# Expert outputs scattered without accumulation and summed at the end, and the first block's down projection moved one expert later

## What is computed

```
scores = sigmoid(xf @ w_router)
_, idx = top_k(masked(scores + router_bias), TOP_K)         # 8 of 64 experts per token
wts = sel / sum(sel) * ROUTED_SCALE
def body(acc, blk):                                         # tok, w: the slots of one expert; e: the expert
    xb = x_pad[tok]
    yb = ((silu(xb @ w_gate[e]) * (xb @ w_up[e])) @ w_down[e]) * w[:, None]
    return acc.at[tok].add(yb), None
h = h + routed + shared                                     # h: the residual stream
h = h + (p_i @ w_ple_proj) * sigmoid(rmsnorm(h) @ w_ple_gate)
y = rmsnorm(h)
```

## Time and profile before

| | us |
|---|---|
| median of three runs (lowest, highest) | 1949.45 (1948.63, 1951.06) |
| the profiled execution | 1950.84 |
| its span, first to last instruction | 1949.0 |
| PE busy in the span | 1740.4 |
| DVE, ACT, POOL busy | 885.6, 785.5, 572.5 |
| mean granted TensorE clock, as a share of full speed | 0.951 |

### The profile page before, as it was taken

One profiled execution on the slowest core, in us unless ns is written; L12 is line 12 of the kernel. 1 busy time (PEld: TensorE's weight loads), 2 busy tenths in 40 slices (PEclk: granted clock), 3 DMA queues, 4 the chain that ended last, 5 costly groups with the idle time before them and its releaser, 6 DMA issues. The chain is left out here.

```text
span 1949.0 us, 24720 instructions
## 1 busy us (share of the span) xinstructions
PE 1740.4 (89%) x7154; PEld 1086.3 (56%) x7155; DVE 885.6 (45%) x1566; ACT 785.5 (40%) x1453; POOL 572.5 (29%) x668
## 2 busy tenths in 40 slices
PE   6999999978883989898999998999998989786998
PEld 4666666536772556465555655655555556452443
DVE  3333334316994543554444445444455443552333
ACT  2222222213330554564554555545555454551221
POOL 0011000002554332443333334334334242441010
PEclk9999999978996999999999998999999999897999
DMA  9200000022114889999999899999899898984001
GB/s 357 92 0 0 0 0 0 27 81 110 65 65 145 255 277 270 298 296 297 271 272 293 256 278 324 275 264 297 254 312 305 250 285 253 302 264 137 33 22 38
DMA packets 122124, 371.34 MB, mean 191 GB/s; under 512 B 18674, under 2 KB 33970, under 8 KB 121677
## 3 DMA queue, kind: packets, MB, share of 16 engines
q1 hardware_dynamic: 86021, 257.30, 36.2%
q0 software_dynamic: 35760, 113.69, 24.9%
q10 hardware_dynamic: 320, 0.07, 0.0%
HBM read 298.86 MB, written 74.01 MB: 191 GB/s over the span
## 5 line engine op out<-in xcount | busy, mean ns | idle before, releaser
L1406 PE MATMUL Y<-raw_d,hT 128*128 128x512 f32 (+1 forms) x768 | 367.1, 624 | 20.6 <-ACT hT L1466 19.5
L191 DVE TENSOR_TENSOR lo_gu<-raw_g,hi_gu 128x1024 fp32r<-128x1024 f32 x130 | 154.6, 1223 | 399.5 <-ACT hi_gu L184 399.3
L1322 POOL DMA_INDIRECT acc_dram<-y,to_row x128 | 215.2, 1681 | 402.9 <-ACT y L1474 315.0
L1364 PE MATMUL GU<-hi_gu,x_hi 128*128 128x512 f32 (+1 forms) x768 | 326.2, 425 | 5.7 <-issue 4.1
L1364 PE MATMUL GU<-hi_gu,x_lo 128*128 128x512 f32 (+1 forms) x768 | 308.7, 402 | 0.0
L1364 PE MATMUL GU<-lo_gu,x_hi 128*128 128x512 f32 (+1 forms) x768 | 308.2, 401 | 0.0
L1474 ACT ACTIVATE y<-Y,w_t 128x512 f32<-128x512 f32 (+1 forms) x256 | 168.6, 684 | 253.2 <-PE Y L1406 251.7
L1406 PEld LDWEIGHTS Y<-raw_d,hT 128*128 128x128 f32 (+1 forms) x768 | 137.8, 186 | 189.9 <-issue 174.7
L1364 PEld LDWEIGHTS GU<-hi_gu,x_hi 128*128 128x128 f32 (+1 forms) x768 | 138.9, 181 | 78.6 <-issue 41.6
L107 POOL TENSOR_SCALAR st<-st 128x1 f32<-128x1 f32 (+3 forms) x45 | 9.3, 206 | 571.5 <-ACT junk L579 200.7
L1364 PEld LDWEIGHTS GU<-lo_gu,x_hi 128*128 128x128 f32 (+1 forms) x768 | 137.8, 179 | 48.7 <-issue 12.0
(11 more groups left out here) (219 smaller groups left out, 2059.1 us busy)
## 6 DMA issues: line engine op xcount, KB each, us to landing
raw_g<-in_w_exp_gate SPq DMA_DIRECT2D x130, 512.0 KB, 9.9
raw_u<-in_w_exp_up SPq DMA_DIRECT2D x130, 512.0 KB, 10.4
raw_d<-in_w_exp_down SPq DMA_DIRECT2D x130, 512.0 KB, 5.9
rows_dram<-row SPq DMA_DIRECT2D x9, 512.0 KB, 2.7
acc_dram<-resid SPq DMA_DIRECT2D x9, 512.0 KB, 2.7
w_big<-in_w_in SPq DMA_DIRECT2D x2, 2048.0 KB, 12.6
w_out<-in_w_out SPq DMA_DIRECT2D x1, 4096.0 KB, 19.0
w_big<-in_w_ple_gate SPq DMA_DIRECT2D x64, 64.0 KB
```

The costliest lines, as they stand in the source:

```text
L191: dve.tensor_tensor(part_of(keep, "lo", m, par, h), part_of(keep, "raw", m, par, h), part_of(keep, "hi", m, par, h).bitcast(F32), ALU.subt ...
L1322: pool.indirect_dma_start(out=acc_dram[:, :], out_offset=bass.IndirectOffsetOnAxis(ap=to_row[0:n, b:b + 1], axis=0), in_=y[b][0:n, :], in_ ...
L1364: ins = pe.matmul(out, lhs[x], rhs[w], start=first and i == 0, stop=last and i == 2)
L1406: ins = pe.matmul(Y[half][0:n, :], hT[b][:, f, :], raw_d[par][:, f, cols], start=f == 0, stop=f == FC - 1)
```

## The change

The experts' results are no longer added into `acc_dram` by the DMA. `acc_dram` becomes `h_dram`, which the router writes and the output stage reads. The results go to a new table, `y_dram`, with eight rows for each token, one for each of its experts, so that no two writes meet; the scatter is plain. The list holds 8 times the token plus the choice, and the gathers use that number shifted right by three. Empty slots of both transfers point behind the table's end and are left out by a bounds check, so that the zero rows and their writes are gone. In the output stage SP loads the eight rows of each token (4 MB to a tile, into `yk`, two buffers), and DVE adds them to the residual one after another.

In the experts stage, PE does the `down` of expert m's block 0 during the pass of expert m + 1, in the gaps of that pass; block 1's stays where it was. `hT` of block 0 gets two buffers. The weights `raw_d[1 - par]` are thus read during the following pass, and the initial increment of `y_done[1]` is gone. For the first pass, SP loads expert 0's down weights also into the other buffer and waits for them. After the last pass two halves of `down` and one scatter follow.

```
-            sp.sem_inc(y_done[1], 1)
+            for h in range(2):
+                sp.dma_start(part_of(keep, "raw", "d", 1, h), expert_weights(a, "d", 0, h)).then_inc(ld["d"][h], 16)
+            for h in range(2):
+                sp.wait_ge(ld["d"][h], 16)
+                sp.dma_start(part_of(keep, "raw", "d", 0, h), expert_weights(a, "d", 0, h)).then_inc(ld["d"][h], 16)
...
-            def scatter(b):
+            def scatter(b, m):
                 n = BLK[b]
+                pool_after(pool, keep["passed"], y_st[b], 16 * m + 16)
+                own.did(pool.tensor_copy(to_row[b][0:n, :], to_t[0:n, b, bass.ds(m + b, 1)]))
+                own.wait()
+                pool_after(pool, keep["passed"], y_ev[1], 2 * m + b + 2)
                 pool.indirect_dma_start(
-                    out=acc_dram[:, :], out_offset=bass.IndirectOffsetOnAxis(ap=to_row[0:n, b:b + 1], axis=0),
-                    in_=y[b][0:n, :], in_offset=None, compute_op=ALU.add).then_inc(y_st[b], 16)
+                    out=y_dram[:, :], out_offset=bass.IndirectOffsetOnAxis(ap=to_row[b][0:n, 0:1], axis=0),
+                    in_=y[b][0:n, :], in_offset=None, bounds_check=Y_ROWS - 1, oob_is_err=False).then_inc(y_st[b], 16)
...
             def two_blocks(m, par):
                 gate_up(0, m, par)
                 transposes(1, m)
                 transposes(0, m + 1)
+                down(0, m, 1 - par, 0, 1, (0,))
                 h_transposes(0, m)
                 gate_up(1, m, par)
-                down(0, m, par, 0, 1)
+                down(0, m, 1 - par, 0, 1, (1,))
                 h_transposes(1, m)
-                down(0, m, par, 1, 1)
+                down(0, m, 1 - par, 1, 1)
                 down(1, m, par, 0, 1)
                 down(1, m, par, 1, 1)
...
             def one_block(m, par):
...
                 gate_up(0, m, par)
                 transposes(0, m + 1)
+                down(0, m, 1 - par, 0, 2)
                 h_transposes(0, m)
-                down(0, m, par, 0, 2)
-                down(0, m, par, 1, 2)
+                down(0, m, 1 - par, 1, 2)
...
             sp.dma_start(resid[:, 0, :], rows[:, 0, :]).then_inc(h0_ld, 16)
+            chosen_rows(0, P)
             sp.dma_start(g_ple[:], a["g_ple"][0:1, :].broadcast_to([P, D])).then_inc(out_st, 16)
             sp.dma_start(resid[:, 1:TILES, :], rows[:, 1:TILES, :]).then_inc(h_ld, 16)
             sp.dma_start(g_fin[:], a["g_final"].rearrange("(a d) -> a d", a=1).broadcast_to([P, D])).then_inc(g_ld, 16)
+            chosen_rows(1, P)
...
+            def gather_sum(t, ks, par):
+
+                for k in ks:
+                    if k % (TOP // 2) == 0:
+                        dve.wait_ge(y_ld[par][k // (TOP // 2)], 16 * loads(t))
+                    ins = dve.tensor_tensor(resid[:, t, :], resid[:, t, :], yk[par][:, k, :], ALU.add)
```

More of the change, by code:

```diff
@@ L133, in build, with mid @@
         )
[L134 to L147, removed]
+        with ExitStack() as middle:
+            def mid(name, shape, dt=F32):
+                return middle.enter_context(nc.sbuf_tensor(name, shape, dt))
+            keep |= dict(raw_g=mid("raw_g", [P, KC, FE]), raw_u=mid("raw_u", [P, KC, FE]), raw_d=[mid("raw_d0", [P, FC, D])])
+            with ExitStack() as front:
+                keep["resid"] = front.enter_context(nc.sbuf_tensor("resid", [P, TILES, D], F32, side="right"))
+                mixer(nc, a, o, c, keep, o_dram, list_dram)
+                keep |= dict(
+                    rounds=mid("rounds", [1, 1], I32),
+                    fill=mid("fill", [1, PAIRS], I32),
+                    to_t=mid("to_t", [P, 2, PAIRS + 3], I32),
+                    idx_t=mid("idx_t", [P, 2, PAIRS + 3], I32),
+                    w_t=mid("w_t", [P, 2, PAIRS + 1]),
+                    hi_gu=[mid("hi_gu0", [P, 2, KC, FE], F32R)], lo_gu=[mid("lo_gu0", [P, 2, KC, FE], F32R)],
+                )
+                router(nc, a, c, keep, rows_dram, h_dram, list_dram)
+            keep["ple"] = ctx.enter_context(nc.sbuf_tensor("ple", [P, TILES, PLE], F32, side="right"))
+            experts(nc, a, c, keep, rows_dram, y_dram)
+        output(nc, a, o, keep, h_dram, y_dram)
 ROUTER_LOADS = 10
@@ L1332, in pair @@
                 gather(0, m + 2)
[L1334 to L1341, removed]
+                scatter(0, m)
+                scatter(1, m)
                 own.clear()
@@ L1347, in _ @@
                     y_st[b], 16)
+            for b in range(2):
+                own.did(pool.memset(rows[b][:], 0.0))
+            own.wait()
             gather(0, 0)
@@ L1396, in h_transposes, with down @@
                 ins.then_inc(h_tr[b], 1)
-            def down(b, m, par, half, counts):
+            def down(b, m, par, half, counts, fs=range(FC)):
                 n = BLK[b]
-                pe.wait_ge(h_ev[b], m + 2)
-                pe.wait_ge(y_ev[half], 2 * m + b + 1)
                 cols = slice(half * 512, (half + 1) * 512)
[L1403 to L1407, removed]
+                if fs[0] == 0:
+                    pe.wait_ge(h_ev[b], m + b + 1)
+                    pe.wait_ge(y_ev[half], 2 * m + b + 1)
+                for f in fs:
+                    if half == 0:
+                        pe.wait_ge(ld["d"][f], 16 * m + 16 * b + 16)
+                    ins = pe.matmul(Y[half][0:n, :], hT[b][par][:, f, :], raw_d[par][:, f, cols], start=f == 0, stop=f == FC - 1)
+                if fs[-1] == FC - 1:
+                    ins.then_inc(y_done[half], counts)
             def two_blocks(m, par):
@@ L1437, in pair @@
                     one_block(m, par)
-            pe.wait_ge(blank, 3)
+            pe.wait_ge(blank, 4)
             transposes(0, 0)
             each_pair(pe, pair)
+            m = pe.value_load(rounds[0:1, 0:1], min_val=1, max_val=ROUNDS) * E
+            for half in range(2):
+                down(0, m, 1, half, 1)
         @block.scalar
@@ L1494, in _ @@
                 act.sem_inc(h_ev[half], 1)
-            act.wait_ge(blank, 3)
+            act.wait_ge(blank, 4)
             x_high(0, 0)
             each_pair(act, pair)
+            m = act.snap(act.value_load(rounds[0:1, 0:1], min_val=1, max_val=ROUNDS) * E)
+            for half in range(2):
+                weighted(0, m, half)
         @block.vector
```

141 lines of the change are left out of this document (78 added, 63 removed).

## The result

The changed kernel took **2395.36 us** (median of four runs, 2392.44 to 2406.81) against 1950.26 for the kernel before on the same chip: a ratio of **1.229** (95% interval 1.2251 to 1.233), slower by 23%. The profiled execution is the one of 2406.81 us, with a span of 2404.9. The forecast was 2309, in a range from 2165 to 2425.

A forecast was written before the change was run, and what follows sets the result against it. PE and the DMA engines were taken to run close to full in the experts stage. From 1950.8 us, +264 loop, +62 clock, +29 output stage, +5 edges gave 2311, or 2309 against the median; range 2165 to 2425.

The forecast's parts named there:

- The mechanism: Experts stage: SP's wait for `raw_d` holds up the next expert's loads, closing a loop through ACT and PE; +264 us.
- PE's idle time: Ahead of `h_transposes(0)` in every pass, PE waits 2.6 us with two blocks and 6.1 with one.
- L: Experts stage: time for all seven of SP's transfers after its release; 12.0 us, bounds 9.5 to 14.3.
- With the queues full [...] so 10.1 us: Step for the burst: weights and scatters, together 3.77 MB, move at an average of 372 GB/s, so 10.1 us.
- the prediction's first rival: Experts stage: transfers run at their best rate, 406 to 420 GB/s, L = 11.1, 2230 us in all; 20 in 100.
- The clock: Experts stage: PE's idle time lowers its clock, costing 2.4 and 2.2 us a pass; +62 us, bounds -85 and +85.
- The output stage: First norm comes 23 us later, tile 1's rows some 2, DVE's chain 4; +29 us, between 15 and 50.
- The edges: Two more halves of `down` at the end, 3.6 us, and router-end shift and copies, about 1; +5 us.
- What it gives is that L holds 0.56 MB and not 0.87: Experts stage: leaving out empty slots only cuts the scatter bytes in the burst, from 0.87 to 0.56 MB.
- its rival: Experts stage: the DMA does not leave out empty slots, 0.87 MB of scatter, L + 0.8, 2362 us; 6 in 100.
- If SP's release doesn't bind: Rival, faster: the experts stage takes 982 us instead of 1120, and the kernel 1846 in all; 4 in 100.
- the idle time of 0.84 goes, a pass has 19.4 and 11.3 us: Faster case, experts stage: PE's 0.84 us gap ahead of `h_transposes` vanishes, giving 19.4 us with two blocks, 11.3 with one.

The follow-up runs named there:

- gate piece last: Changed kernel with the 64 KB of the output stage's weights issued behind `raw_u`, not ahead of `raw_g`; 2390.87 us, ratio 1.2254.
- PE kept busy: Changed kernel with PE's `gate_up` of block 0 computed twice over the same values, loads and their order unchanged; 2343.42 us, ratio 1.2018.
- the run with the scatters alone: Changed kernel with `down` and SP's count back in their old places, plain scatters and output-stage sums kept; 1903.11 us, ratio 0.976.

## Why the prediction was right, and which terms were off

**The mechanism held at each step it named**: the wait at `raw_d` followed at once by the gate pieces, no wait of theirs for `lo_gu`, ACT's splits waiting for the DMA, PE idle ahead of `h_transposes` in every pass, a DMA share of 0.52, and a clock of 0.85. The run with gate and up ahead of the wait shows that it is the cause. PE's idle time was put at 2.6 us with two blocks and 6.1 with one, and is 4.8 and 8.4 on average: 2.2 us more in each, which is what L took more. But it goes by the blocks of the pass before, whose last products stand behind the release, and not by those of the pass itself, as the prediction has it; in passes of either kind the mean is 6.5. The terms can be compared by pass. The table is worked out from the starts in each run's timeline, as means over the 63 passes between its releases, 31 with two blocks and 32 with one: L, from the release to ACT's last split; the rest of a pass, for two blocks and for one; and the time from the release to the first `raw_g` split.

```
kernel                          mean pass     L   rest, two   rest, one   first raw_g
predicted                            22.6  12.0        14.5         6.7           6.3
changed kernel                       24.1  14.2        13.8         6.1           8.8
gate piece last                      23.9  14.0        13.7         6.3           8.4
PE kept busy                         23.0  14.0        12.7         5.4           8.9
gate and up first, same wait         19.4  10.1        13.2         5.5           4.1
no scatters                          21.7  12.3        13.3         5.6           8.2
empty slots written                  24.9  14.9        13.9         6.2           8.8
```

**L is the term that was mis-sized**: 14.2 for 12.0, 64 x 2.2 = 141 us. The step that failed is "With the queues full [...] so 10.1 us", with one start and end of 1.9 for the whole burst. By it the first `raw_g` (1.64 MB with what stands ahead of it) should have been split 6.3 us after the release; it was 8.8, in the run without scatters 8.2. From there on, without scatters, the pieces come 1.4 us apart, as the 1.4 of the prediction has it, and the scatters add 1.9 where 1.5 were counted. So some 2 us are lost between the down weights and the first `raw_g`, in the slump of the windows. It stands in the mean over all passes of the changed kernel: 159 GB/s from 4 to 6 us after the release, with 0.34 us for a packet of 4 KB of SP's queue, and 407 GB/s with 0.16 us from 7.5 to 12. Neither the gate piece nor the scatters make it, since without the one the first `raw_g` comes after 8.4 and without the other after 8.2. In the run with gate and up first, it comes after 4.1, 0.8 more than the best landing of the earlier trace rows, and a slow piece stands later. What makes the slump is not settled.

The slices of the earlier trace rows could have warned of it. Five in a row stand there at 278 to 299, and the prediction's first rival puts such slices down to POOL's transfers. That reading is wrong: in the last two of the five, POOL's queue moved 0.02 of 0.35 MB, while in the slices at 326 to 408 before them, from 622.2 to 624.5 us, it moved 0.74 of 0.89 MB.

An estimate by the Trainium skill (DMA: Bandwidth & Descriptors, "Anatomy of one DMA") stood in the rival of the best rate, with L = 10.6. That section is on transfers issued by GpSimd, and these are SP's. The trace does not bear it out for seven of them issued in a row: the 14.2 measured are further from it than from the forecast.

**The clock was taken too dear.** The rest of a pass at full clock was put at 12.1 and 4.5; it was 13.8 and 6.1, so the clock cost 1.7 and 1.6 us, not 2.4 and 2.2: 32 x 3.3 = 107 for 147, and with the 85 us of before taken off +22 for +62. The run with PE kept busy bears out the base: from `h_transposes` to the release its median is 9.8 and 2.2 us, as the 12.1 and 4.5 less the 2.3 ahead of it. Its means in the table lie higher, since some of its passes start `h_transposes` later or still have the lower clock.

**The output stage** took 25.5 us more (29 forecast), with the first norm 26.3 us after the first wait of the chain began, 6.2 before, 20 more where 23 were forecast, and a period of 18.96 (19 forecast). **The edges**: 456 less 424 and 25.5 leave 6 (5 forecast).

The sum against the profiled execution was 2311. With L +141, the clock -40 and the output stage -3.5 it becomes 2408; 2406.81 was measured. Two errors of opposite sign made the forecast look better than its terms: with L as long as it was and the clock as dear as forecast, it would have been about 2450, outside the range. That much of being right is luck.

**The other statements.** "What it gives is that L holds 0.56 MB and not 0.87": the run with empty slots written has 53.6 us more, as its rival had it (2362 against 2309). "If SP's release doesn't bind", 1846 were expected; the run in which gate and up don't wait for it took 1912. The step that failed there is "the idle time of 0.84 goes, a pass has 19.4 and 11.3 us": the mean is 16.31 and not 15.35, 61 us in all, of which 49 are PE's wait for `hid`, part of it moved to `raw_u`. And plain scatters were put at nothing by themselves in the loop. No run has adding scatters in the loop, so that is not shown; outside it the run with the scatters alone gains 47 us, though its output stage takes 26 more.

## What to carry to other kernels

Where an engine issues loads in program order, a later release of one buffer delays every load behind it, so ask of each wait that moves not what it guards but what stands behind it. If the wait can't be moved, put what is needed first ahead: here that was worth 285 us behind the same wait, and to move the wait behind the urgent loads 483. The price of a transfer's bytes depends on whether something waits for them: the same 20 MB cost 4.5 us, within the intervals, where the loads ran ahead and the DMA share was 0.79, and 53.6 us where each pass waited for its loads.

## What was unexpected of the hardware

- Transfers issued back to back did not keep their rate: 150 GB/s for 2 us in the middle of a burst that reached 416, and by the table some 2 us lost ahead of the first `raw_g` of a pass on average, with the gate piece elsewhere and, in another run, with the scatters gone as well.
- Adding scatters cost more than their bytes: the queue took 24.9% of the engines' time for 113.69 MB before, 13.1% for 92.39 MB when the rows were written plainly, and its 4 KB packets 0.30 and 0.16 us in the median. The Trainium skill (DMA: Bandwidth & Descriptors, "Rules for kernel authors") says that an accumulating DMA reads its destination and writes it later; the rows agree with a dearer write, though they can't show the read by itself.
